# Three seven-product groups per gated layer in place of two, in a float32 kernel that splits every weight

## The chip, the cores and the metric

The kernel runs on one core of a Trainium2 chip, as one launch. The metric is the device time of that launch in microseconds. Its engines are TensorE (PE, and PEld for its weight loads), VectorE (DVE), ScalarE (ACT), GpSimd (POOL) and SyncE (SP), which here only issues the loads of the weights.

## The reference

Two transformer blocks follow each other on a sequence of 256 tokens of width 1024, all in float32. The first block has two attentions and a convolutional feed-forward part. The second has two layers, and in each of them a gated feed-forward part stands ahead of the attention and one behind it: four gated parts in all, called gated layers here. What each computes:

```python
def swiglu(h, wg, wu, wd):
    return (jax.nn.silu(h @ wg) * (h @ wu)) @ wd
...
for l in range(DEPTH_2):
    x = x + 0.5 * rmsnorm(swiglu(h, ffn_wg[l, 0], ffn_wu[l, 0], ffn_wd[l, 0]), g[1])
    ...
    x = x + 0.5 * rmsnorm(swiglu(h, ffn_wg[l, 1], ffn_wu[l, 1], ffn_wd[l, 1]), g[5])
```

`wg` and `wu` are 1024 x 2816 and `wd` is 2816 x 1024.

## The kernel before

**Split products.** Each float32 operand is split into a high part and a low remainder, and each product is three matmuls of 128 x 128 on 128 x 512: high by high, high by low, low by high. Every weight block therefore passes ACT, which copies it to the high part (line 2091, tiles `w_hi`, `hi_qk`, `hi_at`), and DVE, which subtracts to get the low part (line 2360, tiles `w_lo`, `lo_qk`, `lo_at`). Both do it in two halves of 128 x 1024.

**Units and slots.** The weights stream in units of 2048 columns per partition (1 MB). A unit lands in one of three `raw` slots and is split into one of five pairs of split slots. SP loads the next unit into a raw slot when the unit in it is split; a split slot is written again when PE has used it. All engines follow one list of steps in a fixed order, so that each engine takes its steps strictly one after the other; semaphores tie them.

**A gated layer** has 11 chunks (0 to 10) of 256 hidden columns. A plain chunk takes two units of gate and up weights (24 matmuls each, lines 2825 to 2827), then ACT's silu (line 2256) and DVE's product (line 2735), four transposes on PE (line 3106), the split of the result into `hc_hi` (ACT, line 2289) and `hc_lo` (DVE, line 2744), and one unit of down weights (24 matmuls). The down product of a chunk stands in the list about one chunk behind its up product.

**A group** takes two neighbouring chunks at once. Gate and up blocks of 512 columns and the two tiles of 128 tokens form a 2 x 2 by 2 x 2 block product, done with seven block products (`gprod`, 12 matmuls each, lines 3080 to 3082) in place of eight. For it

- DVE forms four sums of weight blocks (line 2352, two halves of 128 x 1024 each, into `scr` or over `raw`), and the group has seven units to split where two plain chunks have four;
- once per layer DVE forms sums of the tokens: line 2389 behind the down product of chunk 0, lines 2397 to 2403 behind chunk 2's up product; ACT copies their high part (line 2261), and DVE makes the low part (line 2406, tile `mixed_lo`), which the group's second product on PE needs;
- ACT and DVE combine the products (lines 2265, 2412 to 2424), and DVE forms the hidden rows (line 2435 and line 2439, once for each tile of tokens), which PE transposes (line 3089, `gturn`). A raw slot whose block is still needed for a sum is held until that sum is split:

```python
pl.release[u1], pl.release[u5] = u5, u7
...
pl.release[u2] = u4
```

**Where groups stand.** `GROUPS` lists the first chunk of each group. The layer's loop takes a group where `c in GROUPS`; if another group ended just before (`close = c - 2 in GROUPS`), the two transposes of that one stand behind the first and the second product of the new one:

```python
product_of(u1, p1, True, tile=(0, 0), mixed=None)
if close:
    self.group_turn(c - 2, 0, banks[3])
product_of(u5, p5, True, tile=None, mixed=3)
```

`tail` does chunk 10. If a group ended just before (`c - 2 in GROUPS`), it puts half of the first up unit, then that group's transposes, then the rest.

Of the kernel before, what the change touches and what calls it, by code (L numbers as in the profile page):

```python
# [47 lines left out]
UNIT = 2048  # L48
RAW, SPLIT, EXTRA = 3, 3, 2
FIRST = 4  # L50
GROUPS = (4, 7)
MORE = 3 * len(GROUPS)
UNITS = 228 + 4 * MORE
WIDE = ((25, 99 + MORE), (113 + MORE, 183 + 3 * MORE), (195 + 3 * MORE, 228 + 4 * MORE))
# [212 lines left out]
def build_plan(W):  # L267
# [505 lines left out]
    class FfnHead(Head):  # L773

        def __init__(self, turn_args, banks0, banks1, up_units, conv, w_down, during=(), before_end=(), gate_up=None):
            Head.__init__(self, turn_args, banks0, banks1)
            self.gate_up = gate_up
            self.singles = [c for c in range(NFC) if conv or not any(g <= c < g + 2 for g in GROUPS)]
            self.during, self.before_end = list(during), before_end
# [99 lines left out]
        def go_on(self):  # L879
# [22 lines left out]
            while c < NFC - 1:  # L902
                if c in GROUPS:
                    self.group(c)
                    c += 2
                    continue
                after_group = c - 2 in GROUPS
                less = 1 if c + 1 in GROUPS else 0
                self.up(c, 0)
# [16 lines left out]
        def group(self, c):  # L926
# [9 lines left out]
            def product_of(u, use, start, **of):  # L936
                pl.split_ahead(u)
                pl.add("gprod", unit=u, use=use, start=start, **of)
# [7 lines left out]
            p1, p5, p7 = (pl.use(b, u) for b, u in zip(banks, (u1, u5, u7)))  # L946
            close = c - 2 in GROUPS
            product_of(u1, p1, True, tile=(0, 0), mixed=None)
# [2199 lines left out]
```

How the kernel before makes its waits and increments, by code:

```python
        def wait_ready(eng, use):  # L1790
            if use.unit is not None:
                eng.wait_ge(unit_used, use.unit + 1)
            else:
                eng.wait_ge(psum_ready[use.bank], use.ready)
# [1 line left out]
        def wait_read(eng, use):  # L1797
            name, value = use.read_by
            eng.wait_ge(psum_read[use.bank] if name == "psum_read" else named[name], value)
# [6 lines left out]
        def wait_past(eng, free):  # L1807
            for f in free:
                if isinstance(f, int):
                    eng.wait_ge(unit_used, f + 1)
                else:
                    wait_ready(eng, f)
# [1 line left out]
        def wait_rows(eng, what):  # L1815
            if what in raw_slot:
                eng.wait_ge(weight_loaded[raw_slot[what]], landed[what])
                return raw[:, raw_slot[what], :]
            e = plan.early.index(what[1])
            eng.wait_ge(early_landed[e % FIRST], 16 * (e // FIRST + 1))
            return early_rows[e % FIRST]
# [56 lines left out]
        @block.sync  # L1879
# [3 lines left out]
            def wait_consumed(number):  # L1883
                if isinstance(plan.ada_done[number], int):
                    sp.wait_ge(ada_used, plan.ada_done[number])
                else:
                    wait_ready(sp, plan.ada_done[number])
# [4 lines left out]
                    e = plan.early.index(what[1])  # L1892
                    if e == 2:
                        sp.wait_ge(c_act_ready, 1)
                    if e >= FIRST:
# [38 lines left out]
            def link(ins):  # L1934
                pool.wait_ge(pool_step, mark(ins))
```

## Time and profile before

| | |
|---|---|
| median of 3 runs | 1410.62 us (1409.11 to 1411.71) |
| profiled execution, its own time | 1411.21 us |
| its span, first to last instruction | 1409.5 us |
| mean granted TensorE clock | 0.992 |
| PE busy | 1375.7 us (98%), 6957 matmuls |
| DVE busy | 1096.6 us (78%) |
| ACT busy | 817.3 us (58%) |
| four gated layers | each about 176 us, from 439, 747, 935 and 1233 us |

The busy share of PE counts matmuls that overlap in its pipeline, so that its pace is read from the starts of neighbouring matmuls and not from their durations. Idle time of DVE or ACT counts only if somebody waits for them.

### The profile page before, as it was taken

Reading aid. Unit: us, or ns where it says so; the run is one execution under the profiler, and the core shown is the slowest. Engines: PE = TensorE matmul, PEld = TensorE weight load, DVE = VectorE, ACT = ScalarE, POOL = GpSimd, SP = SyncE. Lnnn points to the kernel's source line nnn. Section 1 sums busy time; section 2 is a strip of 40 time slices with the busy share of each in tenths; the row PEclk is TensorE's granted clock in tenths of the full one; section 3 lists DMA queues with packets and bytes.
Section 4 is the critical chain, followed back from the end, with each engine's and each line's share of the span. In section 5 each row is a group of like instructions: output and inputs, shape, how many; then the busy total and the mean of one; then the engine's idle time right before and its main releaser. Section 6 shows DMA issues by size and latency. Waiting matters only on the chain.

```text
span 1409.5 us, 19422 instructions
## 1 busy us (share of the span) xinstructions
PE 1375.7 (98%) x6957; PEld 1143.3 (81%) x6957; DVE 1096.6 (78%) x1563; ACT 817.3 (58%) x1305; POOL 80.7 (6%) x133
## 2 busy tenths in 40 slices
PE   6999999999999999999899999999999999999998
PEld 5878877999987888887678888888888877788886
DVE  6577787799767999669986999569996556779893
ACT  4556755755446466466576566465655566566562
POOL 3011100000000000012300000000000100000000
PEclk8999999999999999999999999999999999999999
DMA  9887555487553574635255566735747373564560
GB/s 352 300 292 252 194 178 182 146 282 258 189 194 127 193 239 162 236 131 171 98 169 170 174 220 208 239 106 197 249 152 263 118 222 120 178 221 131 203 239 30
DMA packets 160702, 274.37 MB, mean 195 GB/s; under 512 B 5953, under 2 KB 87617, under 8 KB 160609
## 3 DMA queue, kind: packets, MB, share of 16 engines
q1 hardware_dynamic: 153904, 250.86, 52.2%
q0 software_dynamic: 5552, 20.20, 4.6%
q10 hardware_dynamic: 1153, 2.07, 0.4%
q8 instruction: 57, 0.93, 0.3%
q14 instruction: 36, 0.29, 0.1%
HBM read 272.05 MB, written 1.06 MB: 194 GB/s over the span
## 4 chain that ended last, share of the span: by engine, by line
PE 73%; DVE 7%; issue 2%; ACT 1%; DMA 1%; POOL 0%; DVEq 0%; POOLq 0%; ACTq 0%; SPq 0%
PE psum L2825 18%; PE psum L2827 17%; PE psum L2826 17%; PE psum L3080 3%; PE psum L3081 3%; PE psum L3082 3%; PE psum L2868 2%; PE psum L2867 2%; PE psum L2865 2%; DVE w_lo L2360 2%; PE psum L3106 1%; PE psum L2930 1%; DVE lo_at L2360 1%; PE psum L3002 1%; DVE lo_qk L2360 1%
## 5 line engine op out<-in xcount | busy, mean ns | idle before, releaser
L2360 DVE TENSOR_TENSOR w_lo<-raw,w_hi 128x1024 fp32r<-128x1024 f32 (+2 forms) x310 | 368.0, 1231 | 70.6 <-ACT w_hi L2091 69.5
L2091 ACT ACTIVATE w_hi<-raw 128x1024 fp32r<-128x1024 f32 (+2 forms) x310 | 307.9, 1047 | 94.0 <-DMA raw<-in_ffn_wu_dram 25.3
L2825 PE MATMUL psum<-w_hi,hT_hi 128*128 128x512 f32 x712 | 287.4, 404 | 3.2 <-DVE hT_lo L2522 1.2
L2826 PE MATMUL psum<-w_lo,hT_hi 128*128 128x512 f32 x712 | 278.9, 392 | 0.0
L2827 PE MATMUL psum<-w_hi,hT_lo 128*128 128x512 f32 x712 | 278.9, 392 | 0.0
L2825 PEld LDWEIGHTS psum<-w_hi,hT_hi 128*128 128x128 f32 x712 | 135.0, 190 | 35.8 <-issue 7.1
L2827 PEld LDWEIGHTS psum<-w_hi,hT_lo 128*128 128x128 f32 x712 | 134.9, 190 | 29.1
L2826 PEld LDWEIGHTS psum<-w_lo,hT_hi 128*128 128x128 f32 x712 | 135.1, 190 | 25.8 <-issue 0.5
L2825 PE MATMUL psum<-w_hi,hc_hi 128*128 128x512 f32 x272 | 106.7, 392 | 0.9 <-DVE hc_lo L2744 0.6
L2827 PE MATMUL psum<-w_hi,hc_lo 128*128 128x512 f32 x272 | 106.0, 390 | 0.0
L2826 PE MATMUL psum<-w_lo,hc_hi 128*128 128x512 f32 x272 | 106.0, 390 | 0.0
L2360 DVE TENSOR_TENSOR lo_at<-raw,hi_at 128x1024 fp32r<-128x1024 f32 x74 | 87.3, 1219 | 8.0 <-ACT hi_at L2091 7.9
L2360 DVE TENSOR_TENSOR lo_qk<-raw,hi_qk 128x1024 fp32r<-128x1024 f32 (+1 forms) x72 | 84.0, 1206 | 4.8 <-ACT hi_qk L2091 4.6
L2091 ACT ACTIVATE hi_at<-raw 128x1024 fp32r<-128x1024 f32 x74 | 74.3, 1050 | 21.7 <-PE psum L2827 5.8
L2091 ACT ACTIVATE hi_qk<-raw 128x1024 fp32r<-128x1024 f32 (+1 forms) x72 | 71.4, 1041 | 21.2 <-DMA raw<-in_ffn_wu_dram 7.5
L2031 POOL TENSOR_TENSOR stat<-stat,minus_half 128x1 f32<-128x1 f32 (+2 forms) x24 | 17.4, 726 | 1116.5 <-DVE stat L2502 1042.2
L2256 ACT ACTIVATE PR<-psum,stat 128x256 f32<-128x256 f32 x56 | 24.1, 472 | 71.7 <-PE psum L2827 70.5
L2825 PEld LDWEIGHTS psum<-w_hi,hc_hi 128*128 128x128 f32 x272 | 51.1, 188 | 12.7 <-DVE hc_lo L2744 1.6
L2827 PEld LDWEIGHTS psum<-w_hi,hc_lo 128*128 128x128 f32 x272 | 51.0, 188 | 10.8
L2826 PEld LDWEIGHTS psum<-w_lo,hc_hi 128*128 128x128 f32 x272 | 51.1, 188 | 10.0
L2121 ACT ACTIVATE hT_hi<-psum,cols 128x128 fp32r<-128x128 f32 x96 | 27.4, 368 | 51.8 <-PE psum L2930 51.8
L2289 ACT ACTIVATE hc_hi<-psum 128x512 fp32r<-128x512 f32 (+1 forms) x32 | 17.2, 539 | 67.2 <-PE psum L3106 67.2
(301 smaller groups left out, 2871.6 us busy)
## 6 DMA issues: line engine op xcount, KB each, us to landing
raw<-in_ffn_wd_dram SPq DMA_DIRECT2D x44, 1024.0 KB, 4.8
raw<-in_ffn_wg_dram SPq DMA_DIRECT2D x56, 512.0 KB, 3.9
raw<-in_ffn_wu_dram SPq DMA_DIRECT2D x56, 512.0 KB, 5.4
raw<-in_w_up_dram SPq DMA_DIRECT2D x44, 512.0 KB, 4.8
raw<-in_w_in_dram SPq DMA_DIRECT2D x19, 1024.0 KB, 7.6
raw<-in_ffn_wg_dram SPq DMA_DIRECT2D x16, 1024.0 KB, 5.1
raw<-in_ffn_wu_dram SPq DMA_DIRECT2D x16, 1024.0 KB, 5.2
ada_raw<-in_w_ada_dram POOLq DMA_DIRECT2D x24, 512.0 KB, 5.3
```

What stands on the lines that cost most here:

```text
L2091: nc.scalar.activation(hi_of(s)[:, cs], source_of(s)[:, cs], ACT.Copy).then_inc(ready, 1)
L2121: ins = nc.scalar.activation(tiles_of(hT_hi, k0 + i, 1, a["ts"])[:, 0, :], psum[:, a["use"].bank, i * w:(i + 1) * w], ACT.Copy, scale=g)
L2360: nc.vector.tensor_tensor(lo_of(u)[:, cs], source_of(u)[:, cs], hi_of(u)[:, cs].bitcast(F32), ALU.subtract)\
L2825: nc.tensor.matmul(o, a_hi, b_hi, start=start, stop=False)
L2826: nc.tensor.matmul(o, a_hi, b_lo, start=False, stop=False)
L2827: return nc.tensor.matmul(o, a_lo, b_hi, start=False, stop=stop)
L2865: nc.tensor.matmul(o, hi[:, b], hT_hi[:, kk, :], start=kk == 0 and f % 2 == 0, stop=False, skip_group_check=True)
L2867: nc.tensor.matmul(o, hi[:, b], hT_lo[:, kk, :], start=False, stop=False, skip_group_check=True)
L2868: ins = nc.tensor.matmul(o, lo[:, b], hT_hi[:, kk, :], start=False, stop=kk == KT - 1, skip_group_check=True)
L3080: nc.tensor.matmul(o, a_hi, b_hi, start=a["start"] and k == 0, stop=False, skip_group_check=True)
L3081: nc.tensor.matmul(o, a_hi, b_lo, start=False, stop=False, skip_group_check=True)
L3082: ins = nc.tensor.matmul(o, a_lo, b_hi, start=False, stop=k == 3, skip_group_check=True)
```

## The change

The first chunks of the groups become 3, 6 and 8 in place of 4 and 7. So chunks 3,4 and 6,7 and 8,9 are groups, 5 and 10 are plain behind groups, the third group follows directly upon the second, and chunk 10 takes the branch of `tail` for a group just before. All else, the order of steps and the numbering of units and slots, follows from these numbers.

```diff
-GROUPS = (4, 7)
+GROUPS = (3, 6, 8)
 MORE = 3 * len(GROUPS)
 UNITS = 228 + 4 * MORE
```

The first place is on DVE in the first gated layer, from the low parts of units ahead of the first group to the low part of the token sums. Tiles: `w_lo`, `lo_at`, `lo_qk` are low parts of weights, `scr` or `raw` written by line 2352 are sums of weight blocks, `gate_rows` are the token sums, `mixed_lo` their low part. Before:

```order
L2360 TENSOR_TENSOR lo_at<-raw,hi_at 128x1024 x2
L2389 TENSOR_TENSOR gate_rows<-hT_hi,hT_lo 128x1024 x2
L2744 TENSOR_TENSOR hc_lo<-psum,hc_hi 128x512
L2360 TENSOR_TENSOR lo_qk<-raw,hi_qk 128x1024 x2
L2360 TENSOR_TENSOR w_lo<-raw,w_hi 128x1024 x2
L2735 SCALAR_TENSOR_TENSOR PR<-psum,stat,PR 128x256 x2
```

And at that place now:

```order
L2352 TENSOR_TENSOR scr<-raw 128x1024 x2
L2360 TENSOR_TENSOR lo_at<-raw,hi_at 128x1024 x2
L2389 TENSOR_TENSOR gate_rows<-hT_hi,hT_lo 128x1024 x2
L2744 TENSOR_TENSOR hc_lo<-psum,hc_hi 128x512
L2352 TENSOR_TENSOR raw<-raw 128x1024 x2
L2360 TENSOR_TENSOR lo_qk<-scr,hi_qk 128x1024 x2
L2735 SCALAR_TENSOR_TENSOR PR<-psum,stat,PR 128x256 x2
```

Two sums of weight blocks came in, and there is one low part fewer. Between the end of these rows and line 2406 stand, before and now alike, lines 2397 to 2403, one sum (line 2352), one low part and one line 2744.

The second place is on PE, just behind the transposes of chunk 2 in the same layer. Before, the two units of the plain chunk 3 come next (48 matmuls), and the group behind them and one down unit:

```order
L3106 MATMUL psum<-cst,PR 128x128 x4
L2825 MATMUL psum<-hi_at,hT_hi 128x512
L2826 MATMUL psum<-lo_at,hT_hi 128x512
L2827 MATMUL psum<-hi_at,hT_lo 128x512
```

Now the group's first product follows at once, and 12 matmuls later the second, on `mixed_hi` and `mixed_lo`:

```order
L3106 MATMUL psum<-cst,PR 128x128 x4
L3080 MATMUL psum<-hi_at,hT_hi 128x512
L3081 MATMUL psum<-lo_at,hT_hi 128x512
L3082 MATMUL psum<-hi_at,hT_lo 128x512
```

The third place is on DVE where the third group follows upon the second. The rows begin behind lines 2412 to 2420 of the second group and end at its hidden rows (line 2439, first tile of tokens), which PE's transposes need. Before, behind the second group comes a plain chunk:

```order
L2360 TENSOR_TENSOR w_lo<-raw,w_hi 128x1024 x4
L2424 TENSOR_TENSOR gate_rows<-psum,gate_rows 128x512
L2360 TENSOR_TENSOR lo_at<-raw,hi_at 128x1024 x2
L2439 SCALAR_TENSOR_TENSOR PR<-gate_rows,stat,PR 128x512
L2360 TENSOR_TENSOR lo_qk<-raw,hi_qk 128x1024 x2
L2435 TENSOR_TENSOR gate_rows<-psum,gate_rows 128x512
L2439 SCALAR_TENSOR_TENSOR PR<-gate_rows,stat,PR 128x512
```

Now:

```order
L2352 TENSOR_TENSOR scr<-raw 128x1024 x2
L2360 TENSOR_TENSOR lo_at<-raw,hi_at 128x1024 x2
L2352 TENSOR_TENSOR raw<-raw 128x1024 x2
L2360 TENSOR_TENSOR lo_qk<-scr,hi_qk 128x1024 x2
L2424 TENSOR_TENSOR gate_rows<-psum,gate_rows 128x512
L2352 TENSOR_TENSOR scr<-raw,scr 128x1024 x2
L2360 TENSOR_TENSOR w_lo<-raw,w_hi 128x1024 x2
L2439 SCALAR_TENSOR_TENSOR PR<-gate_rows,stat,PR 128x512
L2360 TENSOR_TENSOR w_lo<-scr,w_hi 128x1024 x2
L2435 TENSOR_TENSOR gate_rows<-psum,gate_rows 128x512
L2439 SCALAR_TENSOR_TENSOR PR<-gate_rows,stat,PR 128x512
```

Three sums for the third group now stand ahead of the second group's first row of line 2439.

## Rows read from the trace of the kernel before

**Rows 1.** The page: busy us (share of the span) and instructions of each engine.

```profile
PE 1375.7 (98%) x6957; PEld 1143.3 (81%) x6957; DVE 1096.6 (78%) x1563; ACT 817.3 (58%) x1305; POOL 80.7 (6%) x133
```

**Rows 2.** Waits of PE: us in total, times, longest; whole trace.

```profile
PE psum L2891 <- DMA PR<-in_b_conv_dram: 7.3, 1, 7.3
...
PE psum L3089 <- DVE PR L2439: 0.3, 1, 0.3
```

**Rows 3.** Windows, gated layers 1 and 2: length; PE, PEld, DVE, ACT, POOL busy; clock; DMA.

```profile
439.00:615.00 176.00, 175.39 (x805) 144.72 (x805) 141.21 (x162) 101.42 (x139) 1.50 (x3) 1.00 0.57 192
747.00:923.00 176.00, 175.70 (x799) 144.85 (x798) 143.18 (x157) 100.33 (x129) 1.89 (x3) 1.00 0.57 194
```

**Rows 4.** Timeline of PE, first gated layer: start us, us, instruction; behind chunk 2.

```profile
475.76 0.49 PE L3106 MATMUL psum<-cst,PR 128*128 128x128 f32 x3
476.01 0.48 PE L2825 MATMUL psum<-hi_at,hT_hi 128*128 128x512 f32 x1
...
477.26 0.39 PE L2827 MATMUL psum<-hi_at,hT_lo 128*128 128x512 f32 x1
...
479.98 0.39 PE L2827 MATMUL psum<-hi_at,hT_lo 128*128 128x512 f32 x1
```

**Rows 5.** Timeline of DVE, first gated layer, up to the token sums' low part.

```profile
461.43 2.36 DVE L2360 TENSOR_TENSOR lo_at<-raw,hi_at 128x1024 fp32r<-128x1024 f32 x2 [0.88 <-ACT hi_at L2091]
463.71 2.35 DVE L2389 TENSOR_TENSOR gate_rows<-hT_hi,hT_lo 128x1024 f32<-128x1024 f32 x2
...
471.12 0.87 DVE L2735 SCALAR_TENSOR_TENSOR PR<-psum,stat,PR 128x256 f32<-128x256 f32 x2
471.90 0.68 DVE L2397 TENSOR_TENSOR gate_rows<-gate_rows 128x512 f32<-128x512 f32 x1
...
474.68 2.35 DVE L2352 TENSOR_TENSOR scr<-raw 128x1024 f32<-128x1024 f32 x2
...
480.04 0.68 DVE L2744 TENSOR_TENSOR hc_lo<-psum,hc_hi 128x512 fp32r<-128x512 f32 x1
480.64 2.28 DVE L2406 TENSOR_TENSOR mixed_lo<-gate_rows,mixed_hi 128x2048 fp32r<-128x2048 f32 x1
```

**Rows 6.** Timeline of ACT in the same stretch.

```profile
463.29 2.01 ACT L2091 ACTIVATE hi_qk<-raw 128x1024 fp32r<-128x1024 f32 x2 [0.54 <-DMA raw<-in_ffn_wu_dram]
...
474.79 1.92 ACT L2261 ACTIVATE mixed_hi<-gate_rows 128x2048 fp32r<-128x2048 f32 x1 [3.55 <-DVE gate_rows L2403]
```

**Rows 7.** Timeline of DVE through the first group and up to the second.

```profile
508.37 0.68 DVE L2412 TENSOR_TENSOR gate_rows<-psum,gate_rows 128x512 f32<-128x512 f32 x1
...
510.29 2.35 DVE L2360 TENSOR_TENSOR lo_qk<-raw,hi_qk 128x1024 fp32r<-128x1024 f32 x2
...
522.46 0.76 DVE L2439 SCALAR_TENSOR_TENSOR PR<-gate_rows,stat,PR 128x512 f32<-128x512 f32 x1 [0.79 <-ACT PR L2275]
524.43 2.36 DVE L2352 TENSOR_TENSOR scr<-raw 128x1024 f32<-128x1024 f32 x2 [1.21 <-DMA raw<-in_ffn_wu_dram]
...
528.98 1.28 DVE L2444 TENSOR_TENSOR hc_lo<-psum,hc_hi 128x512 fp32r<-128x512 f32 x2
...
542.16 0.69 DVE L2744 TENSOR_TENSOR hc_lo<-psum,hc_hi 128x512 fp32r<-128x512 f32 x1 [1.86 <-ACT hc_hi L2289]
```

**Rows 8.** DMA issues from 440 to 600 us: KB each, median us to landing.

```profile
raw<-in_ffn_wd_dram SPq DMA_DIRECT2D x10, 1024.0 KB, 4.8
...
raw<-in_ffn_wu_dram SPq DMA_DIRECT2D x4, 1024.0 KB, 6.1
```

**Rows 9.** Timeline of PE behind its longest wait after the first 20 us.

```profile
86.01 1.10 PE L2913 MATMUL psum<-ada_acc,ones 128*128 128x512 f32 x2 [3.18 <-issue]
...
87.30 0.63 PE L2826 MATMUL psum<-w_lo,hT_hi 128*128 128x512 f32 x1
...
90.28 0.47 PE L2827 MATMUL psum<-w_hi,hT_lo 128*128 128x512 f32 x1
90.59 0.39 PE L2825 MATMUL psum<-w_hi,hT_hi 128*128 128x512 f32 x1
```

## The prediction

> **What bounds the kernel now.** The page first: PE is busy 98% of the span, PEld 81%, DVE 78%, ACT 58% [rows 1]. Then PE's waits: the longest, 7.3 us, is for the first loads; for DVE's group rows the list has 0.3 us in all four gated layers, behind line 2439 [rows 2]. So PE practically never waits there, and its pace sets the end: from 477.26 to 479.98 us it starts 12 matmuls, which is 2.72 us, or 0.227 us each [rows 4]. The windows show how near DVE is: of 176 us it works 141 and 143 in the first two gated layers, at full clock [rows 3]. PE is fed from a stock: five split slots, each worth 5.44 us of PE in a plain chunk (24 matmuls), but only 2.72 us in a group. DVE takes 2.27 us for a low part of a unit or a sum of blocks (461.43 to 463.71, [rows 5]). In a group it must make seven low parts and four sums, 25 us, while PE needs 19 us for its seven products. A group lives on the stock.
>
> **What the change removes.** Each gated layer has one group more: 84 matmuls in place of 96. 12 x 0.227 = 2.7 us per layer, 10.9 us in all. The transposes stay eight for a pair of chunks.
>
> **What it adds.** Per added group, three more units to split and four sums, 7 x 2.27 = 15.9 us of DVE; and its combining rows (lines 2412 to 2420 1.92 us [rows 7], then lines 2424, 2435 and twice 2439 at 0.7 to 0.8 us) in place of lines 2735 and 2744, some 3 us more. So 19 us of DVE for 2.7 us less of PE. I go through the first gated layer with the new order and these durations, PE and DVE side by side, and look where DVE is late.
>
> *First wait: the low part of the token sums.* PE reaches the transposes behind chunk 2 at 475.76 us as before, since nothing ahead of them changed, and the group's first product begins at 476.01 [rows 4]. The second product reads `mixed_lo`. Before, a plain chunk, a down unit and the first product lay between: PE began it at about 495.6, and line 2406 ended at 480.64 + 2.28 = 482.92 [rows 5]. Now PE is there at 478.8. DVE: the low part ahead of line 461.43 ends at 461.43 - 0.88 = 460.55. The new sum needs the load that ACT's row shows landed at 463.29 [rows 6]. From there: sum, low part, line 2389, 3 x 2.27, 470.1; line 2744 0.60 (480.04 to 480.64), 470.7; second sum, low part, 475.3; line 2735 0.78, 476.1; lines 2397 to 2403 2.8, 478.9; third sum, 481.2. The next low part waits for ACT, which copies the token sums first (1.92, [rows 6]) and then a half unit (1.0, half of 2.01): 481.9. Low part 484.2, line 2744 484.8, line 2406 **487.1**. The down unit of chunk 1 now starts 0.6 us late (its `hc_lo` is ready at 470.8, PE is there at 470.3), so PE stands from 479.4 to 487.1: **7.7 us**. Bound from below: only two sums more and a low part less, 482.92 + 2.27 = 485.2, against 479.2: 6.0 us.
>
> *Second wait: the second group's transposes, behind the third group's first product.* PE from 487.1: 14 group products (38.1), 6 units of 24 (32.7), 12 transposes (1.1): 559.0, and 1.5 for the small wait where the first group's transposes meet line 2439: 560.5. DVE from 487.1 to line 2439 of the second group: the new order has 20 low parts and 8 sums, 63.6; the combining of group one 5.7 (with the 0.79 that line 2439 waits for ACT) and of group two 3.4; lines 2444, 2735 and 2744 2.6 [rows 5, 7]: 562.4. Before, DVE lost 1.21 there on a load and 1.86 on ACT [rows 7]; with them and 0.2 for handing over, 565.7. PE waits **5.2 us**; without them 1.9 us. Three of the eight sums are the third group's, which its neighbour now has ahead of line 2439.
>
> *Third wait: the third group's transposes inside chunk 10.* PE from 565.8: 6 group products (16.3), 2 down units (10.9), half an up unit (2.7), transposes (0.7): 596.4, plus 1.5 at the second set of transposes of the second group: 598. DVE from 565.7: six low parts and a sum 15.9, line 2435 to line 2439 2.25, lines 2444 1.2, lines 2412 to 2420 1.92, an ACT wait 1.4: 588.4. By `release` the raw slot of the last gate block is free only now, and in it goes the down weights' load: issue 0.4, landing 4.8 [rows 8], half a copy 1.0: 594.6. Then three low parts 6.8, line 2439, line 2435 and line 2439 3.05: 604.5. PE waits **6.5 us**; 3 if the load hides.
>
> Small waits: 0.6 + 1.5 + 1.5 = 3.6, less what was there before, 0.5. Per layer 7.7 + 5.2 + 6.5 + 3.1 - 2.7 = **+19.8 us**.
>
> *The clock.* After its wait of 3.18 us PE ran nine 512-column matmuls at 0.43 us each (87.30 to 90.28 is seven steps) before it was back at 0.23 [rows 9]: the level of 1.2 GHz in place of 2.4, and 1.9 us lost. Each of the three waits is longer than that. Behind the first two the loss is mostly taken back by the next wait, since DVE has not waited with PE; behind the third it stays: +1.9, and 0.3 of the others. Per layer **+22 us**, four layers +88. The other three start from the same state: their window's DVE time is alike.
>
> Sum against the profiled execution: 1411.2 + 88 = **1499 us**. That execution is 0.6 us above the median, which is nothing here. A change under 0.2% (3 us) could not be told from none.
>
> A page speaks for the change. The Trainium skill, Perfetto Trace Analysis, section Identifying the Most-Contended Engine, says to find the engine of highest occupancy (for TensorE by its weight loads) and to optimize it first. By that rule PE's relief should show: 1400 us. The rows agree on which engine it is; whether DVE's share of a whole span says enough is what differs.
>
> **The rivals.**
> *The stock covers it all, faster.* PE drops 10.9 us and nobody is late: 1411.2 - 10.9 = 1400.3 us, -0.8%. For it: the shares; DVE would go from 1096.6 to 1096.6 + 4 x 19 = 1173 us, 84% of 1400, still below PE. Against it: the token sums. It decides at PE's 478.8 us; line 2406 ended at 482.92 even in the old order, with fewer rows ahead of it. 3%.
> *Only the token wait.* If PE's standing lets DVE fill the slots and that stock lasts to chunk 10: 6.0 + 1.9 - 2.7 = +5.2 per layer, 1432 us. Against it: in the 75 us behind, DVE has no slack by the count. 7%.
> *The loads set the pace.* The group's up blocks landed after 6.1 us and not 4.8 [rows 8]. If each load that DVE waits for costs 1.3 us more, with six such in a layer, it is +30 per layer, 1531 us. For it: sums need a block landed earlier than its copy, and raw slots are held longer. Against it: the bytes are the same, 192 GB/s in such a layer [rows 3]. 10%.
>
> **How the numbers follow.** Forecast as worked out 78%; rivals 3, 7 and 10%; the last 2% half for no change, half for times beyond the third rival. Range: with all lower bounds 6.0 + 1.9 + 3.0 - 2.7 + 1.9 = +10.1 per layer, 1452; the middle between that and the sum is likelier than the end, so 1460 to 1528, just short of the third rival. Faster 3%, same 1%, slower 96%.
>
> **What would show it.** PE: 48 matmuls fewer, and three waits per gated layer: 7 to 8 us ahead of line 3080 on `mixed_hi`, by line 2406; 5 and 6 us ahead of line 3089, by line 2439. DVE busy near 1173 us and 95% and more inside the groups; mean clock near 0.98. The token step is wrong if line 2406 ends before PE's first product does; the other two if line 3089 finds its rows ready, and then the stock was larger than my count. The sum fails if DVE's durations grow beside the denser loads, or if PE's waits are put down to loads.

## The result, and the profile after

| | before | changed |
|---|---|---|
| median of the runs | 1410.82 us (4 runs, 1409.11 to 1411.71) | 1497.95 us (4 runs, 1496.26 to 1500.25) |
| ratio | | 1.0617, 95% interval 1.0604 to 1.063 |
| profiled execution, span | 1409.5 us | 1494.5 us |
| mean granted TensorE clock | 0.992 | 0.974 |

The kernel became 87 us slower, 21.8 us per gated layer on average; the forecast was 1499 us. The page of the changed kernel, first its busy times (engine, us, share of the span, instructions), then its chain:

```profile
PE 1387.9 (93%) x6909; PEld 1146.2 (77%) x6909; DVE 1171.0 (78%) x1631; ACT 846.6 (57%) x1329; POOL 80.9 (5%) x133
...
PE 53%; DVE 16%; issue 7%; DMA 5%; ACT 3%; POOL 0%; DVEq 0%; POOLq 0%; ACTq 0%; SPq 0%
```

PE has 48 matmuls fewer than before [rows 1] and is busy 12 us longer: the matmuls behind the first two waits below start 0.43 us apart in place of 0.227, at the lower clock. DVE has 74 us more work, as forecast, and its share is the same 78% as before. In the chain PE has 53% and DVE 16%, where the page before has 73% and 7%. A reader who compares only the busy shares of the two pages sees nothing of the cause. PE's waits show it (us in total, times, longest):

```profile
PE psum L3080 <- issue: 29.2, 4, 7.3
PE psum L3089 <- DVE PR L2439: 26.1, 8, 3.6
PE psum L3089 <- DVE hc_lo L2444: 9.3, 4, 2.6
...
PE psum L3080 <- ACT PR L2271: 5.7, 4, 1.7
PE psum L2825 <- DVE hc_lo L2744: 4.7, 7, 1.3
```

The rows of lines 3080 and 3089 come four or eight times: they come back in each gated layer. The last row also stands in the kernel before, with 0.8 us in all. For line 2439 the kernel before had 0.3 us in all [rows 2]. In the first gated layer (440 to 640 us) the sum is 7.3 + 6.5 + 2.6 + 1.3 + 1.0 = 18.7 us. The layer became 20.4 us longer (from the first row of line 2735 to the first of line 2784: 155.4 us before, 175.8 us now).

**The first wait**, on PE and on DVE (start, us, instruction, idle time ahead of it):

```profile
484.44 0.77 PE L3080 MATMUL psum<-hi_qk,mixed_hi 128*128 128x512 f32 x1 [7.31 <-issue]
485.01 0.63 PE L3081 MATMUL psum<-lo_qk,mixed_hi 128*128 128x512 f32 x1
```

```profile
460.58 2.36 DVE L2352 TENSOR_TENSOR scr<-raw 128x1024 f32<-128x1024 f32 x2 [2.73 <-DMA raw<-in_ffn_wu_dram]
...
468.00 2.35 DVE L2352 TENSOR_TENSOR raw<-raw 128x1024 f32<-128x1024 f32 x2
...
476.11 2.35 DVE L2352 TENSOR_TENSOR scr<-raw,scr 128x1024 f32<-128x1024 f32 x2
479.18 2.36 DVE L2360 TENSOR_TENSOR w_lo<-raw,w_hi 128x1024 fp32r<-128x1024 f32 x2 [0.72 <-ACT w_hi L2091]
481.46 0.68 DVE L2744 TENSOR_TENSOR hc_lo<-psum,hc_hi 128x512 fp32r<-128x512 f32 x1
482.06 2.28 DVE L2406 TENSOR_TENSOR mixed_lo<-gate_rows,mixed_hi 128x2048 fp32r<-128x2048 f32 x1
```

PE starts 0.1 us after line 2406 ends (484.34). "issue" means only that the profile shows no releaser; DVE's rows give it. PE's neighbouring matmuls then start 0.43 us apart and not 0.227. The clock in the stretches around it (window, PE, PEld, DVE, ACT, POOL busy, clock, DMA):

```profile
475.00:480.00 5.00, 2.14 (x10) 1.43 (x8) 4.24 (x5) 3.78 (x4) 0.00 (x0) 1.00 0.39 157
480.00:485.00 5.00, 0.56 (x1) 0.50 (x2) 5.00 (x5) 5.00 (x7) 0.00 (x0) 0.73 0.44 129
485.00:490.00 5.00, 5.00 (x15) 3.95 (x14) 5.00 (x6) 1.95 (x4) 0.00 (x0) 0.58 0.21 80
```

It fell while PE stood, and 0.58 is near the 1.2 GHz level (0.5). DVE was busy meanwhile, but for the 0.72 us ahead of 479.18 in which it stood for ACT.

**The second wait** is two. PE, then DVE:

```profile
564.25 1.09 PE L3089 MATMUL psum<-cst,PR 128*128 128x128 f32 x4 [3.60 <-DVE PR L2439]
...
571.80 0.66 PE L3089 MATMUL psum<-cst,PR 128*128 128x128 f32 x4 [2.56 <-DVE hc_lo L2444]
```

```profile
558.81 2.36 DVE L2352 TENSOR_TENSOR scr<-raw,scr 128x1024 f32<-128x1024 f32 x2
...
563.36 0.74 DVE L2439 SCALAR_TENSOR_TENSOR PR<-gate_rows,stat,PR 128x512 f32<-128x512 f32 x1
...
568.78 2.36 DVE L2360 TENSOR_TENSOR w_lo<-raw,w_hi 128x1024 fp32r<-128x1024 f32 x2 [0.27 <-ACT w_hi L2091]
571.06 0.68 DVE L2444 TENSOR_TENSOR hc_lo<-psum,hc_hi 128x512 fp32r<-128x512 f32 x1
```

For the second half the prediction had a small wait of 1.5 us at this place, without its cause. Both transposes of a group that has another behind it go to one PSUM bank (`banks[3]`). The second can only begin when line 2444 of the first has read that bank, and line 2444 stands behind a low part in DVE's order.

**The third wait**, inside chunk 10, on PE, DVE and ACT:

```profile
603.05 0.63 PE L3089 MATMUL psum<-cst,PR 128*128 128x128 f32 x4 [2.90 <-DVE PR L2439]
```

```profile
592.90 2.36 DVE L2360 TENSOR_TENSOR lo_at<-raw,hi_at 128x1024 fp32r<-128x1024 f32 x2 [3.28 <-ACT hi_at L2091]
...
602.15 0.75 DVE L2439 SCALAR_TENSOR_TENSOR PR<-gate_rows,stat,PR 128x512 f32<-128x512 f32 x1 [0.79 <-ACT PR L2275]
```

```profile
591.71 2.01 ACT L2091 ACTIVATE hi_at<-raw 128x1024 fp32r<-128x1024 f32 x2 [6.22 <-DMA raw<-in_ffn_wd_dram]
```

ACT stands for the down weights, whose load could not start before the raw slot was released. DVE stands for ACT's copy, and PE in the end for DVE.

### The profile page after: what moved, and what is told of

It is laid out like the page before. It is cut to its first block, busy times and chain, and to the rows that moved or that the text cites. A ratio compares the mean times of both kernels' runs of the same rounds, so it can differ in the third digit from the quotient of the medians.

```text
span 1494.5 us, 19502 instructions
## 1 busy us (share of the span) xinstructions
PE 1387.9 (93%) x6909; PEld 1146.2 (77%) x6909; DVE 1171.0 (78%) x1631; ACT 846.6 (57%) x1329; POOL 80.9 (5%) x133
## 3 DMA queue, kind: packets, MB, share of 16 engines
HBM read 272.05 MB, written 1.06 MB: 183 GB/s over the span
## 4 chain that ended last, share of the span: by engine, by line
PE 53%; DVE 16%; issue 7%; DMA 5%; ACT 3%; POOL 0%; DVEq 0%; POOLq 0%; ACTq 0%; SPq 0%
PE psum L2825 12%; PE psum L2827 12%; PE psum L2826 12%; DVE w_lo L2360 6%; DMA raw<-in_ffn_wd_dram 3%; PE psum L2868 2%; PE psum L2867 2%; PE psum L2865 2%; PE psum L3080 2%; PE psum L3081 2%; PE psum L3082 2%; DMA raw<-in_ffn_wu_dram 2%; DVE scr L2352 2%; DVE lo_qk L2360 2%; DVE lo_at L2360 1%
## 5 line engine op out<-in xcount | busy, mean ns | idle before, releaser
L2360 DVE TENSOR_TENSOR w_lo<-raw,w_hi 128x1024 fp32r<-128x1024 f32 (+1 forms) x312 | 370.3, 1231 | 67.7 <-ACT w_hi L2091 66.7
L2091 ACT ACTIVATE w_hi<-raw 128x1024 fp32r<-128x1024 f32 (+1 forms) x312 | 310.4, 1046 | 101.9 <-DMA raw<-in_ffn_wd_dram 25.7
L2825 PE MATMUL psum<-w_hi,hT_hi 128*128 128x512 f32 (+1 forms) x672 | 273.0, 406 | 3.2 <-DVE hT_lo L2522 1.2
L2827 PE MATMUL psum<-w_hi,hT_lo 128*128 128x512 f32 (+1 forms) x672 | 264.2, 393 | 0.0
L2826 PE MATMUL psum<-w_lo,hT_hi 128*128 128x512 f32 (+1 forms) x672 | 264.1, 393 | 0.0
L2360 DVE TENSOR_TENSOR lo_at<-raw,hi_at 128x1024 fp32r<-128x1024 f32 (+1 forms) x80 | 93.5, 1208 | 19.2 <-ACT hi_at L2091 19.0
L2091 ACT ACTIVATE hi_at<-raw 128x1024 fp32r<-128x1024 f32 (+1 forms) x80 | 79.6, 1041 | 48.5 <-DMA raw<-in_ffn_wd_dram 19.6
L2360 DVE TENSOR_TENSOR lo_qk<-raw,hi_qk 128x1024 fp32r<-128x1024 f32 x64 | 75.5, 1220 | 4.5 <-ACT hi_qk L2091 4.4
L2091 ACT ACTIVATE hi_qk<-raw 128x1024 fp32r<-128x1024 f32 x64 | 64.0, 1051 | 21.6 <-DMA raw<-in_ffn_wu_dram 6.1
L2352 DVE TENSOR_TENSOR scr<-raw,scr 128x1024 f32<-128x1024 f32 x48 | 56.5, 1220 | 0.9 <-issue 0.4
```

The lines of the kernel that those rows point to most:

```text
L2091: nc.scalar.activation(hi_of(s)[:, cs], source_of(s)[:, cs], ACT.Copy).then_inc(ready, 1)
L2352: nc.vector.tensor_tensor(source_of(u)[:, cs], plus[:, cs], minus[:, cs], ALU.subtract).then_inc(sum_ready, 1)
L2360: nc.vector.tensor_tensor(lo_of(u)[:, cs], source_of(u)[:, cs], hi_of(u)[:, cs].bitcast(F32), ALU.subtract)\
L2825: nc.tensor.matmul(o, a_hi, b_hi, start=start, stop=False)
L2826: nc.tensor.matmul(o, a_hi, b_lo, start=False, stop=False)
L2827: return nc.tensor.matmul(o, a_lo, b_hi, start=False, stop=stop)
```

## The experiments

The question behind a right total is whether its terms are right, and whether the waits are costs that could be removed one by one. My theory was that DVE's side (its work, and the order of its rows, with the loads and copies that they wait for) sets when PE goes on. The rivals were: the number of units and their loads; TensorE's clock behind each wait; and each wait as a cost of its own. All times are medians, ratios are against runs of the kernel before on the same chip; the clock is that of the profiled execution.

| run | us | ratio (95% interval) | clock |
|---|---|---|---|
| e1, groups (3, 7) | 1450.85 | 1.0284 (1.0263 to 1.0305) | 0.983 |
| e2, groups (4, 8) | 1427.93 | 1.0115 (1.0098 to 1.0132) | 0.988 |
| e3, groups (4, 6) | 1454.16 | 1.0308 (1.029 to 1.0325) | 0.985 |
| e4, thin sums | 1466.0 | 1.0387 (1.0372 to 1.0403) | 0.982 |
| e5, thin loads | 1472.9 | 1.0438 (1.0419 to 1.0457) | 0.978 |
| e6, both thin | 1437.53 | 1.018 (1.015 to 1.021) | 0.982 |
| e7, filler | 1489.44 | 1.0551 (1.0527 to 1.0575) | 0.988 |
| e8, sums on POOL | 1555.24 | 1.1025 (1.1004 to 1.1045) | 0.957 |
| e9, low part moved up | 1498.84 | 1.0622 (1.0592 to 1.0651) | 0.978 |
| e10, later transposes | 1500.49 | 1.0624 (1.06 to 1.0649) | 0.969 |
| e11, both thin, both moves | 1432.07 | 1.0139 (1.0119 to 1.016) | 0.991 |
| e12, before, thin loads | 1408.62 | 0.9972 (0.9959 to 0.9985) | 0.997 |

### e1 to e3: each new neighbourhood alone, with only two groups

```diff
-GROUPS = (4, 7)
+GROUPS = (3, 7)     # e1
+GROUPS = (4, 8)     # e2
+GROUPS = (4, 6)     # e3
```

> Two groups as before, but the first at chunk 3: GROUPS = (3, 7). PE has the same work as before. If DVE's order sets PE's waits (my theory), the first wait for the low part of the token sums is there alone, 7 to 8 us per gated layer, with the clock's loss behind it: +9 to 10 us per layer, 1449 us. If the loads or the number of units set the pace, nothing changes against before, since units and sums are as many: 1411 us. If the stock covers the place, also 1411.

> GROUPS = (4, 8): the second group ends just ahead of chunk 10, so that its transposes stand inside chunk 10, and no group follows directly upon another; token sums as late as before. My theory: one wait of about 3 us per gated layer ahead of the second transposes of the group, by the last gate rows, +4 us per layer: 1427 us. By the count of units and loads: 1411 us.

> GROUPS = (4, 6): two groups, the second directly upon the first, then four plain chunks. My theory: PE waits some 5 us ahead of the first group's first transposes (its gate rows stand behind the sums of the next group on DVE) and some 3 to 4 us ahead of the second transposes, which use the same PSUM bank: +12 us per layer, 1458 us. By the count of units and loads: 1411 us.

Measured: 1450.9, 1427.9 and 1454.2 us, within 4 us of what the order of DVE's rows gave. PE's longest waits in the first gated layer of e1, e2 and e3 (the 5.3 us of e2 is its longest; its four layers have 13.2 us together, 3.3 each, where 3 were expected):

```profile
PE psum L3080 <- issue: 7.3, 1, 7.3
```

```profile
PE psum L3089 <- DVE PR L2439: 5.3, 1, 5.3
```

```profile
PE psum L3089 <- DVE PR L2439: 4.5, 2, 3.6
PE psum L3089 <- DVE hc_lo L2444: 2.8, 1, 2.8
PE psum L3080 <- ACT PR L2271: 1.3, 1, 1.3
```

All four kernels with two groups, the one before included, have the same matmuls, units, sums and bytes, and differ by up to 43 us. So the place alone, with the number of units unchanged, makes these differences. Whether the three further units of a third group cost anything at a place without waits was not tried. Each of the three neighbourhoods costs by itself: a group ahead of the token sums 39 us (10 per layer), a group ahead of chunk 10 16 us, two groups in a row 43 us, each against the kernel before on the same chip (1411.57 us). Together that is 98 us, and with PE's 10.9 us less 87, as the change measured, though it has a whole group more. I take that for no proof that the three are independent, since e9 and e10 below speak against it.

### e4: less work for DVE in the sums

```diff
                 for half in range(2):
                     cs = half_of(u, half)
+                    if made["no"] % 12:
+                        cs = slice(cs.start, cs.start + P)
```

> The changed kernel with three groups, but eleven of twelve sums of weight blocks per gated layer are done on 128 of the 1024 columns of each half (what the products then compute is not the reference's). Loads, copies, low parts, products and their order are as in the changed kernel. It takes about 0.95 x 22 = 21 us of DVE's work out of each layer. My theory (DVE is the bound in the groups): the waits behind the first go, the first shrinks from 7.3 to about 2 us, and the time is 1400 to 1415 us. If the loads set the pace it stays above 1480 us; if the restart of the clock is the cost, between the two, with the waits still there.

Measured 1466.0 us: of 87 us only 32 came back. DVE's work alone is not the cause, and this expectation was wrong. Its trace says why: with the sums gone, DVE stands more. PE's waits for line 2439 shrink from 26.1 to 6.9 us, the first wait from 29.2 to 21.7, and those at the shared bank grow from 9.3 to 15.2 (lines from 2352 on stand two further down there). PE's waits, then one of DVE's rows:

```profile
PE psum L3082 <- issue: 21.7, 4, 5.4
PE psum L3091 <- DVE hc_lo L2446: 15.2, 4, 4.2
...
PE psum L3091 <- DVE PR L2441: 6.9, 4, 3.0
```

```profile
481.40 2.36 DVE L2362 TENSOR_TENSOR w_lo<-raw,w_hi 128x1024 fp32r<-128x1024 f32 x2 [2.59 <-ACT w_hi L2091]
```

Ahead of the first wait DVE stands 2.87 us for the up weights' load, as in the changed kernel (2.73), since no work ahead of it fell away. Behind the token sums it stands 2.59 us for ACT, which copies them before the next weight block; in the changed kernel a whole sum filled that time but for 0.72 us.

### e5 and e6: shorter loads, alone and with the thin sums

```diff
                 for c0, n, src in parts:
-                    sp.dma_start(view[:, :, c0:c0 + n], src)...
+                    short = "ffn_w" in src.tensor.name
+                    if short:
+                        src = src[:, 0:1]
+                    sp.dma_start(view[:, 0:1 if short else nk, c0:c0 + n], src)...
```

> The changed kernel, with every load of gate, up and down weights of the gated layers cut to its first quarter (one of four or of two blocks is loaded whole or by half, the rest of the raw slot keeps old weights, so the products are not the reference's). All of DVE's, ACT's and PE's work stays. The run before showed that taking 21 us of DVE's work out of each layer gives back only 8, so DVE's own work isn't all. If the load latency behind a held raw slot is the second part, each load lands some 2 to 3 us earlier and the waits shrink: 1455 to 1475 us. If DVE's work alone counts: 1490 us and more. If the loads set the pace: below 1430 us.

> Both at once: eleven of twelve sums on 128 of 1024 columns, and the loads of the gated layers cut to a quarter (the products are not the reference's). If DVE's work and the load latency are the two causes and nothing else, PE is hardly late anywhere but at the token sums: 1400 to 1425 us. If a third thing holds PE (the fixed order of rows, ACT's copies, the shared bank of the transposes), it stays above 1440 us.

Measured 1472.9 us (25 us back), and 1437.5 us with both (60 us back, where the two alone give 32 + 25 = 57; it lies between the two expectations). The loads of the gate and up weights are a quarter of their size and land after 2.1 to 2.6 us in place of 4.5 to 5.5; those of the down weights are only halved, 3.3 in place of 5.0. In e5's first gated layer (lines three further down), the waits behind line 2439 are:

```profile
PE psum L3092 <- DVE PR L2442: 4.7, 2, 3.6
```

The second wait is still 3.6, so that 1.1 is left of the third wait's 2.9: as much less as the down weights' load lands earlier. So the two causes add up. A third thing was left: 29 us above the kernel before with the same thin loads (e12), where PE's work alone would put it 10.9 us below. PE's longest waits in the first gated layer of e6 (lines five further down):

```profile
PE psum L3085 <- issue: 3.9, 1, 3.9
PE psum L3094 <- DVE hc_lo L2449: 2.1, 1, 2.1
```

### e7: matmuls that keep the clock up

```diff
+            def keep_warm(use, times):
+                for _ in range(times):
+                    nc.tensor.matmul(psum[:, use.bank, :], hT_hi[:, 0, 0:P],
+                                     hT_hi[:, 0:2, :].rearrange("p k n -> p (k n)"),
+                                     start=True, stop=True, skip_group_check=True)
...
+                        keep_warm(use, 28)      # first product on the token sums
                         pe.wait_ge(tokens_split, n_mixed[0])
...
+                    if a["c"] + 2 in GROUPS and t == 0:
+                        keep_warm(use, 20)
                     pe.wait_ge(group_hidden, 2 * a["n"] + t + 1)
```

> The changed kernel, with 28 idle matmuls of 512 columns on PE ahead of its wait for the token sums' low part, and 20 ahead of its wait for the first transposes of the second group, so that TensorE's clock does not fall in these waits (4 x 48 matmuls more; results unchanged). If DVE's side sets the pace, the clock's loss is mostly given back by the next wait: 1488 to 1498 us. If the restart at the lower clock is a cost of its own, 3.4 us per layer come back: 1480 to 1484 us.

Measured 1489.4 us, 8.5 us less than the changed kernel, or 2.1 per layer: at the side where the clock's loss is mostly given back by the next wait. What is left of the first wait behind the idle matmuls (line 2886 there), and the product's first matmuls (lines 3090 and 3091):

```profile
477.83 4.02 PE L2886 MATMUL psum<-hT_hi 128*128 128x512 f32 x17
...
482.79 0.51 PE L3090 MATMUL psum<-hi_qk,mixed_hi 128*128 128x512 f32 x1 [0.94 <-DVE mixed_lo L2406]
483.13 0.40 PE L3091 MATMUL psum<-lo_qk,mixed_hi 128*128 128x512 f32 x1
```

The mean clock rose from 0.974 to 0.988, close to the 0.992 before; it still fell behind the shared bank's wait, which is 3.4 us here (0.69 in 570 to 575). The idle matmuls overran the second wait by 0.9 us (PE goes on at 562.15, line 2439 ended at 561.22). In the first gated layer 8.8 us of waits and 48 x 0.227 = 10.9 us of idle matmuls stand where 18.7 us of waits were: PE, which loses less time to the clock, stands 1 us longer.

### e8: two of the four sums on POOL

```diff
+ON_POOL = (2, 3)
...
             def form(u):
...
+                if made["no"] % 4 in ON_POOL:      # on DVE; POOL has the same function for these
+                    return
```

> The changed kernel, with two of the four sums of weight blocks per group (the one for the fourth product and the one for the last) on POOL, which is idle there; nothing is left out. It takes 6 x 2.27 = 13.6 us per layer off DVE, two thirds of what the thin sums did, if DVE keeps its pace beside POOL. POOL's rows of 512 columns took 1.6 us, so a sum takes some 6.4 us there. If the relief counts: 1475 to 1485 us. If the longer latency of the sums (4 us later each) or a slower DVE beside POOL counts for more: 1500 us and above.

Measured 1555.2 us, 57 us more than the changed kernel. POOL's sums (a row is two halves), DVE's rows beside them, and one group of DVE's low parts with the shortest, median and longest, in ns (lines 2397 and on stand 32 further down there, line 2360 is 2392):

```profile
475.06 5.17 POOL L1993 TENSOR_TENSOR scr<-raw,scr 128x1024 f32<-128x1024 f32 x2 [29.23 <-DVE lo_qk L2392]
492.89 6.49 POOL L1993 TENSOR_TENSOR scr<-raw,scr 128x1024 f32<-128x1024 f32 x2 [12.65 <-DMA raw<-in_ffn_wg_dram]
```

```profile
475.63 2.37 DVE L2429 TENSOR_TENSOR gate_rows<-gate_rows 128x512 f32<-128x512 f32 x1
478.04 2.75 DVE L2431 TENSOR_TENSOR gate_rows<-gate_rows 128x512 f32<-128x512 f32 x1
...
497.04 3.43 DVE L2392 TENSOR_TENSOR lo_at<-raw,hi_at 128x1024 fp32r<-128x1024 f32 x1
```

```profile
L2392 DVE TENSOR_TENSOR lo_at<-raw,hi_at x80: 769/1219/3432, 198.9 to 1518.6; 128x1024 fp32r<-128x1024 f32 x78, 128x592 fp32r<-128x592 f32 x2
```

While a half of the sum runs on POOL, one row of DVE lasts 2.4 to 3.4 us in place of 0.7 or 1.2. They end 0.4 to 1.1 us behind the end of POOL's half (477.65, 480.23, 499.38), as if they only ran then. DVE is busy 1198.5 us with 48 instructions fewer, against 1171.0. A sum moved to POOL therefore takes much of DVE's time all the same, and comes later for those that need it: the longest wait of PE for the token sums is 11.1 us here. The 57 us are not divided between the two. The Trainium skill has a reason for the first in Trainium Architecture — The Big Picture, section What this means for kernel authors: only the port pair that DVE and GpSimd share contends inside SBUF, and it is an exclusive lock, not a split of bandwidth. The trace agrees with a lock (3.43 us against 1.22).

### e9 and e10: a wait removed by order alone

```diff
                     pl.add("token_high")
+                    pl.add("token_low")            # e9
...
                 self.hidden_turn(c)
-                if c == 2:
-                    pl.add("token_low")
```

```diff
-            if close:
-                self.group_turn(c - 2, 0, banks[3])
             product_of(u5, p5, True, tile=None, mixed=3)
             if close:
-                self.group_turn(c - 2, 1, banks[3])
-            pl.add("gkeep", use=p1, slot=0)
+                self.group_turn(c - 2, 0, banks[3])
+            else:
+                pl.add("gkeep", use=p1, slot=0)
             product_of(u7, p7, True, tile=None, mixed=2)
+            if close:
+                self.group_turn(c - 2, 1, banks[3])
+                pl.add("gkeep", use=p1, slot=0)
```

> The changed kernel, with the low part of the token sums (line 2406) straight behind their high part, ahead of the low part and of line 2744 that stand before it; nothing is left out. DVE then stands about 2 us until ACT has copied. If each wait of PE is a cost of its own, the first wait shrinks by 4 us per layer: 1481 us. If DVE's side is the bound and waits only move: the first wait shrinks to 3 to 4 us, some 4 us come back later in the layer at a line 3089, and the total rises by the idle 2 us: 1500 to 1507 us.

> The changed kernel, with the second group's two transposes one product later each in the third group (behind its second and third product in place of its first and second); nothing is left out. If each wait is a cost of its own, the waits for line 2439 (3.6 us) and for the shared bank (2.6 us) go: 6 us per layer, 1473 us. If DVE's side is the bound, they turn into a wait of PE at the next down product or low part, with 1 to 2 us per layer won: 1489 to 1494 us.

Measured 1498.8 and 1500.5 us: no gain in either, where the waits as costs of their own promised 17 and 25 us. In e9, whose time is 1 us below what I gave for waits that only move, the first wait is 3.4 us, as meant, and this is PE's list in the same layer (lines one further up):

```profile
PE psum L3088 <- DVE PR L2438: 6.5, 3, 3.6
PE psum L2824 <- ACT PR L2270: 3.8, 1, 3.8
PE psum L3079 <- issue: 3.4, 1, 3.4
PE psum L3088 <- DVE hc_lo L2443: 2.6, 1, 2.6
```

3.8 us of it came back where line 2824 waits for ACT's read of a PSUM bank (line 2270). It was expected at a line 3089. ACT reached that read only behind a copy, which had stood for a load:

```profile
507.90 2.00 ACT L2090 ACTIVATE hi_at<-raw 128x1024 fp32r<-128x1024 f32 x2 [3.71 <-DMA raw<-in_ffn_wd_dram]
```

In the changed kernel that copy had waited 0.71 us, for PE. So it is not DVE's row order alone that holds PE, but also the loads that its rows set free. With two rows of 1.3 and 1.1 us PE's list sums to 18.7 us, as that of the changed kernel. In e10 the 3.6 us shrank to 0.9 and came back as 2.2 us for line 2437 and 1.8 us for line 2446 at the next products, and the shared bank's wait, which was to go, stayed at 2.6. The third wait fell from 2.9 to 0.3, so that the list sums to 17.1 us there, at a lower mean clock (0.969 in place of 0.974). For e10 even the small gain that I expected was not there.

### e11 and e12: the moves with slack, and the control for the loads

e11 is e6 with the edits of e9 and e10. e12 is the kernel before with the edit of e5.

> The kernel with thin sums and thin loads (1437.5 us; products not the reference's) with both moves: the token sums' low part straight behind their high part, and the second group's transposes one product later each. There DVE and the loads have slack, so a removed wait should stay removed: the 3.9 us of the first wait with its clock loss and the 2.1 us at the shared bank go, 1402 to 1412 us. If something else holds PE there, it stays above 1425 us.

> The kernel before, with the loads of the gated layers cut to a quarter as in the changed kernel's run (products not the reference's): what the shorter loads give where PE does not wait. If the gain of 25 us there came from the waits that the change made: 1405 to 1412 us here. If shorter loads give PE something by themselves (its neighbours' access to memory, an earlier start of the layers): below 1400 us.

e12: 1408.6 us, 3.7 less than before, at the middle of what was expected: of the 25 us of e5 about 21 belong to the waits that the change made. e11: 1432.1 us, 5.5 less than e6 and 20 above the range that I expected, where by the expectation something else holds PE. There, too, most of what the moves took away came back. PE's waits in its first gated layer:

```profile
PE psum L3086 <- DVE hc_lo L2450: 2.2, 1, 2.2
PE psum L3095 <- DVE hc_lo L2450: 1.7, 1, 1.7
PE psum L3095 <- DVE PR L2445: 1.2, 1, 1.2
```

(Lines stand six further down; line 3086 is the product's.) All are for DVE's small rows that stand behind low parts. A group without its sums still has seven low parts, 15.9 us, and small rows of some 6 us (lines 2412 to 2444) for DVE, where PE needs 19 us for its products and 1 us for transposes. By that count DVE has no slack inside a group even then. That this is the third thing was worked out from the rows and not tried: a kernel with cheaper low parts did not run.

## Why the prediction was right, point by point

- **That DVE and not PE decides:** right. Shown by e1 to e3, which keep all the work and move only its place, and by e4 and e5, which take work and latency out of DVE's side. But DVE's work by itself is the smaller part: e4 gave back 32 us of 87.
- **First wait:** forecast 7.7 us, measured 7.3. Line 2406 was forecast to end at 487.1; the layer begins 2.9 us earlier in the profile after (first line 2735 at 445.50, not 448.38), so at 484.2, and it ended at 484.34. The rows ahead of it, too, came within 0.2 us of the working.
- **Second wait:** forecast 5.2 us, measured 3.6, and 2.6 for the shared bank a product later. In the shifted time PE was forecast there at 557.6 and line 2439 to let it go on at 562.8; it was 560.65 and 564.25. The cause was as forecast. For the second transposes, which the bank held for 2.6 us, the prediction had 1.5 us as a small wait.
- **Third wait:** forecast 6.5 us, measured 2.9. This is the term that was mis-sized, by PE's side of it. Line 2439 was forecast to end at 604.5 - 2.9 = 601.6 and ended at 602.90. PE was forecast at 595.1 and came at 600.15, 5 us late: 1.5 us of it stood already when the second wait ended, and the rest is mostly the lower clock behind that wait and the bank. The held raw slot was right: ACT stood 6.22 us for that load, which did not hide. The bound "3 if the load hides" does not come out of the prediction's own numbers: without the 6.2 us of issue, landing and copy, line 2439 ends at 598.3, and PE is there at 598, which leaves 0.3 us.
- **Small waits:** forecast 0.6 + 1.5 + 1.5 us. The first was 0.7, and the third is the bank's 2.6. The second, at the first group's transposes, did not come; in its place PE stood 1.3 us for ACT's read of a bank (line 2271).
- **Clock:** forecast 2.2 us per layer in the sum, and what comes back when the clock is kept up in the first two waits is 2.1 (e7). That the two agree is luck, since 1.9 of the 2.2 stood in the wrong place: they were for the third wait, behind which the clock stayed at 1.00; it fell behind the first two. Waits and clock are not separate terms: PE lost 21.3 + 2.7 = 24 us per layer (from the spans) and stood 18.7 of them; the other 5 us are mostly matmuls at the lower clock, and they made the later waits shorter.
- **The sum** was nearer than its terms: +22 us per layer, measured 21.3 in the span. Terms too large (second and third wait) and too small (clock, bank) offset each other. This is luck in part, and in part they are tied: where DVE's side sets when PE may go on, what PE loses ahead it does not wait later. In e7 idle matmuls took the place of 9.9 us of waits, and only 2.1 us per layer came back; in e9 and e10 waits went and the total stayed.
- **The rival of the loads** (1531 us) was wrong as a rival and right in kind: shorter loads give back 21 us of 87, but inside the forecast, since its count of DVE's time already held waits for loads.
- **The rule of occupancy.** By the Trainium skill, Perfetto Trace Analysis, section Identifying the Most-Contended Engine, the engine of highest occupancy is optimized first; relieving PE would, by the prediction's working, have given 1400 us. The measurement went the other way by 98 us. DVE's share of the span was 78% before and is 78% after; it was full in the stretches that count (5.00 of 5.00 us in 480 to 485).

None of the runs that do the whole work beats the kernel before; nearest is e2. e12, which is faster by 3.7 us, leaves out part of the loads.

## What to carry to other kernels

When a change trades work of a full engine for work of one that seems to have room, do not compare shares of the span: lay the two engines' rows side by side from the last point where both agree, and look where the second has its next row ready. And do not price the waits that you find one by one: where one engine's rows and the loads behind them hold the others, moving a wait gave it another place (e9, e10), and less work or less latency on that side shortened the whole (e4 and e5, 32 and 21 us of 87). The place of a group costs as much as work does: with the same two groups, one of them one chunk further on or nearer, it was 16 to 43 us.

## What was not expected of the hardware

- A row of DVE beside one of POOL, both with two float32 inputs from SBUF, ended only behind POOL's half (e8): 2.37 and 2.75 us in place of 0.69, and 3.43 in place of 1.22. A half of a sum (128 x 1024) took POOL 2.4 to 4.4 us, median 3.2.
- The clock did not fall in the third wait of 2.90 us (1.00 in 600 to 605), and fell in the 3.60 us of the second (0.92, then 0.73 in the next 5 us):

```profile
560.00:565.00 5.00, 1.40 (x8) 0.97 (x6) 5.00 (x6) 2.12 (x2) 0.00 (x0) 0.92 0.55 199
565.00:570.00 5.00, 4.24 (x14) 3.06 (x12) 3.94 (x6) 2.99 (x4) 0.00 (x0) 0.73 0.54 202
600.00:605.00 5.00, 2.10 (x13) 1.73 (x12) 3.95 (x5) 3.59 (x5) 0.00 (x0) 1.00 0.73 229
```
